# A two-layer encoder trunk: the first four units on x times scale, the last four down units by halves

## The reference

```python
def rms_norm(x, gain=None):
    y = x * lax.rsqrt(jnp.mean(x * x, axis=-1, keepdims=True) + EPS)
    return y * gain if gain is not None else y

def modulate(h, shift, scale):
    return h * (1 + scale[:, None, :]) + shift[:, None, :]

def swiglu(h, w_gu, w_down):
    g, u = jnp.split(h @ w_gu, 2, axis=-1)
    return (jax.nn.silu(g) * u) @ w_down

cond = jax.nn.silu(c)
for i in range(DEPTH):
    mod = cond @ mod_w[i] + mod_b[i]
    sh1, sc1, g1, sh2, sc2, g2, sh3, sc3, g3 = jnp.split(mod, 9, axis=-1)
    h = modulate(rms_norm(x), sh1, sc1)
    x = x + 0.5 * g1[:, None, :] * swiglu(h, ffn1_w_gu[i], ffn1_w_down[i])
    ...                                    # the mixer
    x = x + 0.5 * g3[:, None, :] * swiglu(h, ffn2_w_gu[i], ffn2_w_down[i])
    x = rms_norm(x, post_gain[i])
```

## Time and profile before

| | us |
|---|---|
| median of three runs (lowest to highest) | 1985.31 (1983.57 to 1985.61) |
| the profiled execution: its time | 1985.01 |
| its span | 1983.2 |
| TensorE busy | 1952.4 (98%) |
| VectorE busy | 1138.5 (57%) |
| ScalarE busy | 716.8 (36%) |
| GpSimd busy | 214.1 (11%) |

### The profile page before, as it was taken

How to read it: one execution, slowest core, us unless ns; L and a number is a source line. 1 busy time by engine, 2 the same in 40 slices (tenths; PEclk the granted TensorE clock), 3 DMA queues, 4 the chain that set the end, 5 groups by cost and what they waited for, 6 DMA issues and landing times.

```text
span 1983.2 us, 23246 instructions
## 1 busy us (share of the span) xinstructions
PE 1952.4 (98%) x8990; PEld 1619.5 (82%) x8990; DVE 1138.5 (57%) x1692; ACT 716.8 (36%) x1056; POOL 214.1 (11%) x246
## 2 busy tenths in 40 slices
PE   7999999999999999999999999999999999999998
PEld 5888888888888888888888888878888888888886
DVE  7665564799857655645864453586554572433334
ACT  5322222464743213224422221356465442222123
POOL 4110100017701100100110000001111000000000
PEclk9999999999999999999999999999999999999999
DMA  8665552322016655622554543223322233323221
GB/s 318 236 219 170 202 191 96 103 90 88 33 64 223 203 183 187 232 83 87 175 200 136 166 159 108 93 98 112 97 85 86 70 104 97 106 85 106 85 90 59
DMA packets 75197, 263.94 MB, mean 133 GB/s; under 512 B 8770, under 2 KB 8898, under 8 KB 75123
## 3 DMA queue, kind: packets, MB, share of 16 engines
q1 hardware_dynamic: 54720, 190.87, 28.7%
q0 software_dynamic: 20256, 72.02, 11.0%
q10 hardware_dynamic: 146, 0.09, 0.0%
HBM read 260.66 MB, written 2.13 MB: 133 GB/s over the span
## 4 chain that ended last, share of the span: by engine, by line
PE 94%; DVE 3%; POOL 1%; issue 1%; ACT 1%; DMA 0%; SPq 0%; DVEq 0%; ACTq 0%; POOLq 0%
PE bank L1392 29%; PE bank L1397 29%; PE bank L1393 29%; PE bank L1800 1%; DVE dve_tmp L953 1%; PE bank L1817 1%; PE bank L1732 1%; PE bank L1576 1%; DVE h_lo L944 1%; PE bank L1578 1%; PE bank L1577 1%; PE bank L1789 0%; PE bank L1707 0%; PE bank L1456 0%; DVE wlo L816 0%
## 5 line engine op out<-in xcount | busy, mean ns | idle before, releaser
L1392 PE MATMUL bank<-h_hi,whi 128*128 128x512 f32 x1808 | 711.5, 394 | 7.5 <-DVE wlo L816 4.5
L1393 PE MATMUL bank<-h_hi,wlo 128*128 128x512 f32 x1808 | 705.5, 390 | 0.0
L1397 PE MATMUL bank<-h_lo,whi 128*128 128x512 f32 x1808 | 593.9, 390 | 0.5 <-POOL h_lo L378 0.5
L481 ACT ACTIVATE whi<-wraw 128x1024 fp32r<-128x1024 f32 x338 | 347.0, 1053 | 267.0 <-PE bank L1397 263.9
L816 DVE TENSOR_TENSOR wlo<-wraw,whi 128x1024 fp32r<-128x1024 f32 x324 | 389.0, 1224 | 59.9 <-ACT whi L481 59.6
L1392 PEld LDWEIGHTS bank<-h_hi,whi 128*128 128x128 f32 x1808 | 340.7, 188 | 81.0 <-issue 6.1
L1397 PEld LDWEIGHTS bank<-h_lo,whi 128*128 128x128 f32 x1808 | 340.1, 188 | 73.1 <-POOL h_lo L378 1.2
L1393 PEld LDWEIGHTS bank<-h_hi,wlo 128*128 128x128 f32 x1808 | 340.8, 189 | 68.9
L1392 PE MATMUL bank<-hid_hi,whi 128*128 128x512 f32 x832 | 324.3, 390 | 0.0
L1397 PE MATMUL bank<-hid_lo,whi 128*128 128x512 f32 x832 | 323.7, 389 | 0.0
L1393 PE MATMUL bank<-hid_hi,wlo 128*128 128x512 f32 x832 | 323.7, 389 | 0.0
(11 more groups left out here) (237 smaller groups left out, 1351.3 us busy)
## 6 DMA issues: line engine op xcount, KB each, us to landing
wraw<-in_w_units_dram SPq DMA_DIRECT2D x306, 512.0 KB, 3.5
arena<-in_mod_t_dram POOLq DMA_DIRECT2D x96, 512.0 KB, 5.0
mod_tile<-in_mod_t_dram POOLq DMA_DIRECT2D x32, 512.0 KB, 4.8
wraw<-in_w_units_dram SPq DMA_DIRECT2D x32, 384.0 KB, 3.6
arena<-in_mod_t_dram SPq DMA_DIRECT2D x12, 512.0 KB, 8.1
arena<-in_w_units_dram SPq DMA_DIRECT2D x10, 512.0 KB, 4.5
xT<-in_xt_dram SPq DMA_DIRECT2D x8, 256.0 KB, 4.5
sq<-k_roots POOLq DMA_DIRECT2D x8, 256.0 KB, 3.5
```

Of the source, the lines that this page charges most:

```text
L481: act.activation(whi[:, s % RING, :, :], wraw[:, s % RING, :, :], ACT.Copy).then_inc(hi_ready, 1)
L1392: pe.matmul(dst, whi[:, w, k, :], hi_, start=first, stop=False)
L1393: pe.matmul(dst, wlo[:, w, k, :], hi_, start=False, stop=False)
L1397: return pe.matmul(dst, whi[:, s % RING, k, :], lo_, start=False, stop=last)
```

## The change

At the start. `first_tile` orders the tiles so that the eight scales come first and the eight shifts after them. `first_units` works on x times scale: ScalarE rounds it (`first_scaled`), VectorE lowers it (`first_lower`). The root comes by `spread` behind the k = 2 part, ScalarE copies it to `ssum`, and VectorE multiplies it on when it reads the four banks (`first_evict`). The shift's share of the four units is made on TensorE: 16 matmuls with the split shifts as weights and the four weight units as 512 moving columns give two rows, and four small ones turn these into columns (`shift_out`). The full normalised h is made after that, for units 4 and 5 (`first_pair`), whose weights are split into `hid_hi` and `hid_lo`, since the four slots are still in use; units 6 and 7 are split into slots 2 and 3 on VectorE in `ffn`, at the second gate operation.

At the end. `last_units` runs down units 4 to 7 first for tokens 0 to 255 and then for tokens 256 to 511, 18 matmuls of 256 columns each. The statistic, root and products of the first half stand among the units of the second. The root is a ScalarE square root, a reciprocal and one correction step on VectorE in place of GpSimd's power. Sixteen stores of half tiles go out, four of them from ScalarE's queue. In all FFNs the second loop body of the first third is written out.

```diff
 def first_tile(t):
-    return KT * (1 - t % 2) + t // 2
+    return KT + t if t < KT else t - KT
...
+            first_lo(2)
+            first_lo(3)
+            pool.wait_ge(hi_ready, 5)
+            pool.wait_ge(lo_ready, 4)
+            pool.tensor_tensor(first_lo_[0], wraw[:, 0, :, :], first_hi[0].bitcast(F32), ALU.subtract).then_inc(lo_ready, 1)
             for k in range(KT):
-                if k == 1:
-                    first_lo(2)
-                    first_lo(3)
                 pool.wait_ge(h_rounded, k + 1)
...
             hi(0)
+            first_scaled(0)
             hi(1)
-            first_h(0)
+            first_scaled(1)
             hi(2)
             hi(3)
-            for k in range(1, KT):
+            for k in range(2, KT):
+                first_scaled(k)
+                if k == 3:
+                    act.wait_ge(rb_ready, 1)
+                    act.activation(ssum[:, :], bank[RB], ACT.Copy).then_inc(rb_kept, 1)
+            first_raised(0)
+            first_raised(1)
+            for k in range(KT):
                 first_h(k)
+            act.wait_ge(rows_done, 1)
+            hi(6)
+            hi(7)
             act.wait_ge(mod_done, MOD_FIRST)
...
+            def first_lower(k):
+                dve.wait_ge(early_rounded, k + 1)
+                dve.scalar_tensor_tensor(out=h_lo[:, k, :], in0=xT[:, k, :], scalar=modc[:, KT + k:KT + k + 1],
+                                         in1=h_hi[:, k, :].bitcast(F32), op0=ALU.mult, op1=ALU.subtract)\
+                    .then_inc(early_ready, 1)
...
+            def first_evict(n):
+                dve.wait_ge(unit_done, n + 2 - n % 2)
+                dve.tensor_tensor(first_out[n], bank[n], ssum[:, :], ALU.mult).then_inc(evicted, 1)
...
+            for k in range(2, KT):
+                mod_column(k)
+                dve.wait_ge(mod_done, k + 1)
+                first_lower(k)
+            for t in range(KT, MOD_FIRST):
+                mod_column(t)
...
+                        elif f == t == 0 and n < 2:
+                            dve.wait_ge(evicted, s + 2)
+                            dve.wait_ge(shift_kept, 1)
+                            dve.scalar_tensor_tensor(out=dve_tmp[:, n, :], in0=first_out[2 * n + 1],
+                                                     scalar=shift_out[:, 2 * n + 1:2 * n + 2], in1=act_tmp[:, n, :],
+                                                     op0=ALU.add, op1=ALU.mult).then_inc(early_gated, 1)
+                            if n:
+                                lo(6)
+                                lo(7)
...
+            def last_roots(h):
+                at = slice(2 * h, 2 * h + 2)
+                v, y, t, u = var[:, 0, at], rstd[:, 0, at], rstd[:, 0, 4:6], rstd[:, 0, 6:8]
+                dve.wait_ge(stat_done, 7 + h)
+                dve.tensor_scalar(v, bank[OB][:, at], 1.0 / D, EPS, ALU.mult, ALU.add).then_inc(var_ready, 1)
+                dve.wait_ge(deviation_ready, h + 1)
+                link(dve.reciprocal(t, deviation[:, at]))
+                link(dve.tensor_tensor(u, t, t, ALU.mult))
...
+                for n, d, h in last_units():
+                    add_last(n, d, h)
+                    if pending:
+                        sum_square(*pending)
...
+                    if h == 1 and d == WHOLE:
+                        last_roots(0)
+                    if h == 1 and d == KT - 2:
+                        results(0, 0, 2)
+                results(0, 2, 5)
+                last_roots(1)
+                results(0, 5, KT)
+                results(1, 0, KT)
...
                 for k in range(KT):
                     last = part(0, k)
-                    if k:
-                        part(2, k - 1)
                     if k == KT - 1:
                         last.then_inc(unit_done, 2)
+                    if k == 2:
+                        pe.wait_ge(root_ready, 1)
+                        spread(bank[RB], 0, 0).then_inc(rb_ready, 1)
+                    if k:
+                        part(2, k - 1).then_inc(early_used, 1)
                 part(2, KT - 1).then_inc(unit_done, 2)
+                pe.wait_ge(first_shift, 1)
+                rows = bank[OB][0:2, :].rearrange("p (u n) -> p u n", u=4)
+                for k in range(KT):
+                    for m, weights in enumerate((whi, wlo)):
+                        ins = pe.matmul(rows, shift_split[:, k, :], weights[:, 0:4, k, :], start=(k == m == 0),
+                                        stop=(k == KT - 1 and m == 1))
+                ins.then_inc(rows_done, 1)
```

More of the change, by code:

```diff
@@ L71, in third_units @@
     return base, base + 2 * THIRDS[t][1]
+HALF = SEQ // 2
+WHOLE = KT // 2
+LAST_DOWN = third_units(3, 2)[1]
 def up_tiles(f, t, pair):
@@ L178, in shift_at, with fourth @@
             return shift_out[:, n:n + 1]
+        def fourth(whole, u):
+            return whole[:, 4 + 2 * u:6 + 2 * u, :].rearrange("p a n -> p (a n)").rearrange("p (k n) -> p k n", k=KT)
+        first_hi, first_lo_ = [fourth(hid_hi, u) for u in range(2)], [fourth(hid_lo, u) for u in range(2)]
+        first_full = [piece(n * SEQ, SEQ) for n in range(2)]
+        first_out = [sq[:, 0, :], sq[:, 1, :], piece(D, SEQ), piece(D + SEQ, SEQ)]
+        first_rows = piece(5 * D, SEQ)[0:2, :]
         ahead = [piece(0, D), piece(D, D)]
@@ L1061, in ffn @@
                                 mod_column(m)
+                    elif f == 3:
+                        last_down(down, gate)
                     else:
                         down_stats(down, st, gate)
[L1065 to L1070 removed]
             def mask_rows(J, S, b, bias, scale):
@@ L1470, in stat_sums @@
                                         start=False, stop=True, skip_group_check=True)
-                if st not in NORM:
-                    keep_warm(2)
-                    pe.wait_ge(sq_ready, KT * (SUMS_BEFORE[st] + 1))
-                    for b in range(NB):
-                        ins = pe.matmul(bank[OB][:, b:b + 1], sq[:, 1, b * P:(b + 1) * P], ones[:, 0:1], start=False,
-                                        stop=True, skip_group_check=True)
                 ins.then_inc(stat_done, 1)
```

282 lines of the change are left out of this document (221 added, 61 removed).

## The result

The changed kernel takes 2001.11 us (median of six runs, 2000.61 to 2001.50) and the kernel before 1984.44 us (median of six, 1983.16 to 1985.61). The ratio is 1.0083, with a 95% interval of 1.0073 to 1.0093: slower by 14.5 to 18.5 us. The profiled execution took 2001.08 us, its span is 1999.3.

A forecast was written before the change was run, and what follows sets the result against it. TensorE, busy 98% of the span, was taken as the bound, so a later start of units 6 and 7 lengthens the kernel. 1985.0 + 15.5 (late splits) + 2.4 (clock) - 2.5 (end) = 2000.4 us, range 1993 to 2005.

The forecast's parts named there:

- Step 1: Start of the opening: TensorE begins at 17.3 us, 2.85 sooner, then stands until 25.3 for splits of units 2 and 3.
- Step 2: Root in the opening: its copy holds VectorE 5.8 us; eighth lower tile ends at 42.0, four units at 47.7.
- Step 3: Eight shift columns in one piece: split at 51.9 us, TensorE waits 4.2, first normalised tile at 53.9.
- Step 4: Normalised h on ScalarE and GpSimd: 1.45 us a tile, last h_hi at 65.4, last h_lo at 66.8.
- Step 5: Splits of units 6 and 7 queue on VectorE behind gates and columns: start at 77.5, not 61.97, +15.5 us.
- The clock after the wait: TensorE's clock falls in the idle time before units 6 and 7: +2.4 us, from nothing to 6 us.
- The end: Half-width down units and the shorter tail after the matmuls: -2.5 us, bounds -3.7 to -1.2.
- A: Rival: units 6 and 7 are ready when TensorE wants them, the opening chain being far shorter; 1982.7 us, 5%.
- B: Rival: the clock rises soon after 25.3 us and does not fall again; 1995.5 us, 15%.
- C: Rival: the clock stays low longer, 7.5 us; 2002.4 us, or 2005 with a slow tail of 12.3 us; 12%.
- D: Rival: weight loads are not hidden in the end's half units, 10 us more there; 2010 us, 3%.

The follow-up runs named there:

- e4: The changed kernel with ScalarE's copy of the spread root moved from behind its 4th scaled tile to behind its 8th: 1996.17 us.
- e3: The changed kernel with roundings and splits of units 6 and 7 moved up into the norm chain: 2000.18 us, ratio 1.0077 to the kernel before.
- e5: The changed kernel with 34 useless 512-column matmuls between the first pair and units 6 and 7, where TensorE stood 8.2 us: 2000.15 us.
- e7: The changed kernel with the eight subtractions for the norm's lower parts (h_lo) on VectorE instead of GpSimd: 2000.65 us.
- e11: The changed kernel with the norm's product reading the broadcast root from its PSUM bank instead of ScalarE's SBUF copy: 2000.15 us.
- e9: The changed kernel with 10 useless 512-column matmuls where TensorE stands 2.9 us for the splits of units 2 and 3: 1999.03 us.
- e2: The changed kernel's opening with the last FFN of the kernel before: 2003.37 us, ratio 1.0096 to the kernel before.
- e8: The edits of e6 and e7 together in the changed kernel: 1986.05 us, ratio 1.0005 to the kernel before.
- e1: The kernel before with only the changed end (last FFN, last norm, stores), nothing of the opening: 1982.54 us, ratio 0.9988.
- e6: The changed kernel with e3, e4 and the first two gates' four modulation columns moved behind the splits of units 8 and 9: 1987.54 us.
- e12: The kernel of e6 with the norm's product reading the root from its PSUM bank, as in e11: 1985.35 us.
- e10: The kernel of e8 with the same 10 useless matmuls as in e9: 1985.50 us, ratio 1.0003 to the kernel before.

## Why the prediction was right, point by point

Step 1 (first matmul 17.3, stand until 25.3): 17.14 and 25.27. Right.

Step 2 (spread ends 31.4, VectorE stands 5.8 us, eighth lower 42.0, four units 47.7): the copy starts at 30.76, the stand is 5.06, the eighth lower ends at 41.26 and the units end at 47.12. The mechanism was right, and e4 showed that the stand was worth its length to the whole. The size was off by 0.7 us because I let the low clock last 5 us, and it lasted 3.5; e3, e5 and e7 show 5 to 6 us in the same place, so that the 5 was within what this stretch does.

Step 3 (split 51.9, wait 4.2 us, first norm tile 53.9): 51.28, 4.21 and 53.14. The 16 row matmuls took 5.9 us (51.34 to 57.23), because the clock had fallen: between my 3.6 and 6.9.

Step 4 (1.45 us a tile, last h_hi 65.4, last h_lo 66.8): wrong in its price. The chain went at 1.72 us a tile (ScalarE's full tiles at 53.17 and 65.20, seven steps), the last h_hi ended at 66.58 and the last h_lo at 67.96. I took ScalarE and GpSimd for the bound and VectorE's product at before's 0.75 us. But the change also takes the product's operand from the bank to the copy in SBUF, one word in the diff that I passed over; with it the product takes 1.78 us beside GpSimd and is the slowest link. With the bank as operand the chain goes at 1.48 (e11), which is my price. From the first norm tile to the last h_lo I had 12.9 us (53.9 to 66.8), and it took 14.8 (53.14 to 67.96): an error of 1.9 us, which hid step 2's of -0.7. I took the price from a row whose operands were others than those of the new code.

Step 5 (tiles wait until 72.0, splits done 77.45, start 77.5, +15.5): no wait for the tiles, which were there when VectorE came to them at 72.24; that error of 0.75 us and step 2's made up for most of step 4's: the splits are done at 77.66 and the unit starts at 77.72, +15.75. e3 showed the queue as the bound: moved past two gates, the splits of the next pair were late instead. So the path was right, but that +15.5 came out within 0.3 us is partly luck: three terms were off by 0.7 to 1.9 us and fell against each other.

The clock after the wait (+2.4, bounds 0 to 6): 18.58 - 15.75 = 2.83, and 2.70 in e5, where the wait stayed and only the clock was kept. It is not a fixed price: from the start of units 6 and 7 to their silu pass 13.99 us in after, but 12.81 in e4, 13.4 to 13.7 in e7, e9 and e11 and 14.12 in e2, all behind gaps of 6.3 to 8.4 us, against the 11.29 of e5. So the wait cost from 1.5 to 2.8 us, and my 2.4 is within. That the clock falls at all in mid-kernel I had only argued; the traces now show it behind gaps of 2.9 and 3.2 us (after, e3), 4.2 and 8.2. The rule of the Trainium skill that I cited ("TensorE: Matmul & The Clock Gate", section "What's actually happening"), that an idle array is put back to 1.2 GHz, agrees with these rows.

What I did not see is that the fall need not come in the gap itself. In e9 the first three matmuls behind the gap of 4.21 us are still at the full clock, and it falls with TensorE at work; the granted clock is 0.52 from 50.8 to 54.1 us:

```profile
49.78 0.40 PE L1860 MATMUL bank<-whi,shift_split 128*2 128x512 f32 x1 [4.21 <-DVE shift_split L1323]
...
50.80 0.63 PE L1860 MATMUL bank<-whi,shift_split 128*2 128x512 f32 x1
```

In e8 it is the same behind the first gap (2.64 us): three matmuls of 0.50, 0.39 and 0.39 us from 25.42, then 0.63.

The end (-2.5, bounds -3.7 to -1.2): -2.75 in after's profile, -2.43 in e1's, 2.3 between the medians of e2 and after. I left TensorE's clock out of this sum: over before's root and spread it was low and in e2 it was not, which is worth 0.8 us (see e1). Of its terms a matmul of 256 columns took 0.120 us (0.1175 taken), a product of 256 columns 0.34 (0.34), and the root 1.78 us from the variance to its split (1990.69 to 1992.47; 2.1 taken for the stretch).

The sum by the trace: 1985.01 + 18.58 - 2.75 = 2000.84, against 2001.08 of the profiled execution.

The rivals. A (units 6 and 7 ready in time, 1982.7): even with the stands taken out by hand they are done 4.3 (e6), 3.25 (e8) and 2.8 us (e12) later than before (silu at 77.46, 76.38 and 75.90 against 73.13). A counted only TensorE's work. What it left out is the second pass of h through VectorE and ScalarE behind the 16 columns; these three kernels all have it. B (no fall of the clock): fell. C (clock low longer): not in after; e3, e5 and e7 show its first half, at the root (the 12.3 us in it are the slow run of the earlier trace rows). D (weight loads not hidden): excluded by 0.12 us a matmul.

What stays open: why the clock is back at 28.7 us in some executions and only near 31 in others. The traces show the same work ahead of it, and one thing that goes with it. Where full-clock matmuls show already from 20.1 to 21.7 us, ahead of the gap (e3, e5, e7, e11, e12), the clock is low from the first matmul behind it and back only at 30 to 32. Where it rose just before the gap, or no matmul ahead of the gap shows it high (after, e2, e4, e6, e8), it is back at 28.7 to 29.5. What sets the moment, no run here shows.

## What to carry to other kernels

When TensorE starts earlier, the engine to add up is the one that paces it: here the change gave VectorE 13.3 us more busy time (5.2 of them the longer product) in an opening that its queue already set, and the first matmul's gain of 3 us became a loss of 19. Where an operand moves from PSUM to SBUF and GpSimd works beside, its operation has to be priced anew (e11: 0.75 against 1.78 us). A wait that is moved away from one unit must be followed through the queue to the next pair (e3: 8.2 us gone, 4.4 back with a second fall of the clock); only when the queue behind it was cleared too did the sum come down (e6, 13.6 us below after, of which the later root copy alone is 4.9, e4). And two independent changes in one are worth timing apart: the end alone is faster than before, which the whole had hidden.

## What the runs showed of the hardware

- A VectorE product of 128x512 beside GpSimd's subtraction took 1.78 us at the median with both tensor operands in SBUF (after) and 0.746 us with one of them in a PSUM bank (e11); without GpSimd, both in SBUF, 0.745 (e7). GpSimd's subtraction took 1.36 us beside the first and 1.30 beside the second. A weight split on VectorE (128x1024, two SBUF operands) that began just behind a subtraction of GpSimd took 2.29 us (e3 at 67.73, e6 at 62.21). One that began while GpSimd stood idle took 1.21 (e3 at 63.20), and there the two subtractions behind it took 3.66 us together.
- TensorE's clock was at 1.2 GHz behind gaps of 2.9 and 3.2 us, 4.2 us and 8.2 us; behind 1.40 and 1.57 us (e10) it was not. Behind 2.64 (e8) and 4.21 us (e9) it was still at the full level for three matmuls and fell only then, while TensorE worked. It came back 3.3 to 3.5 us after the work in some places (e4 at 76.6, after at 28.7) and about 6 us after it in others (after at 83.4, e3 near 31.7), in the same place later in one trace than in another.
- Matmuls that serve nothing kept the clock up over 8.1 us at no cost that the trace shows (e5): the unit behind them began when its splits were ready (79.42 and 79.48 us), and its pair was 2.70 us shorter.
